# Order of two attention output products, and the place of three weight splits, in a single-core transformer kernel

## What is computed

```
h = rmsnorm(x) * (1 + scale) + shift          # scale, shift from c through w_ada
cq, ckv, k_rope, fq, fk, fv, f_logit, g_mla, g_fox = split(h @ w_in)
o_mla = softmax attention, 8 heads (q and k from cq, ckv through w_uq, w_ukv)
o_fox = forgetting attention, 8 heads (fq, fk, fv, cumulative log gates)
y = sigmoid(g_mla) * (o_mla @ w_o_mla) + sigmoid(g_fox) * (o_fox @ w_o_fox)
x = x + gate_m * (y @ w_out)
```

## Time and profile before

| | |
|---|---|
| runs of the kernel | 1003.09, 1003.9, 1007.6 us; median 1003.9 |
| profiled execution | 1004.27 us, span 1002.5 us |
| TensorE matmul, weight load | 955.7 us (95%), 669.5 us (67%) |
| VectorE, ScalarE, GpSimd | 464.3 us (46%), 378.2 us (38%), 28.3 us (3%) |
| mean granted TensorE clock | 0.993 |
| moved by DMA | 309.37 MB, 309 GB/s on the mean |
| chain that ended last | TensorE 76%, DMA 15%, VectorE 5%, ScalarE 1%, GpSimd 1%, issue 1% |

### The profile page before, as it was taken

How to read it: one execution, slowest core, us unless ns; L and a number is a source line. 1 busy time by engine, 2 the same in 40 slices (tenths; PEclk the granted TensorE clock), 3 DMA queues, 4 the chain that set the end, 5 groups by cost and what they waited for, 6 DMA issues and landing times.

```text
span 1002.5 us, 15338 instructions
## 1 busy us (share of the span) xinstructions
PE 955.7 (95%) x6343; PEld 669.5 (67%) x6343; DVE 464.3 (46%) x860; ACT 378.2 (38%) x718; POOL 28.3 (3%) x60
## 2 busy tenths in 40 slices
PE   7999999898999999999999899999999999898987
PEld 5898778898999999988987434343434344332433
DVE  2797766476787468667875311212121212110113
ACT  2455556554666356454672412121212111110211
POOL 1000000000000000002120000000000000000000
PEclk9999999998999999999999899999999999999999
DMA  9967853633654454534758699999999999999996
GB/s 384 402 266 290 336 203 132 221 120 141 261 187 169 177 204 166 199 138 173 282 218 303 263 430 427 427 427 428 428 428 428 427 428 427 428 427 428 428 425 269
DMA packets 23399, 309.37 MB, mean 309 GB/s; under 512 B 2592, under 2 KB 3104, under 8 KB 4000
## 3 DMA queue, kind: packets, MB, share of 16 engines
q1 hardware_dynamic: 23184, 307.32, 75.3%
q10 hardware_dynamic: 144, 1.05, 0.3%
HBM read 307.31 MB, written 1.05 MB: 308 GB/s over the span
## 4 chain that ended last, share of the span: by engine, by line
PE 76%; DMA 15%; DVE 5%; ACT 1%; issue 1%; POOL 1%; DVEq 0%
PE ps L1001 74%; DMA work<-experts 4%; DMA ring<-experts 4%; DMA slot<-experts 4%; DMA ring<-dense 2%; DVE wl L1656 1%; DMA early<-dense 1%; PE ps L1212 1%; PE ps L1583 1%; DMA colT<-cols 1%; POOL rstd L535 0%; ACT wh L580 0%; PE ps L1525 0%; PE ps L1177 0%; DVE xT L2094 0%
## 5 line engine op out<-in xcount | busy, mean ns | idle before, releaser
L1001 PE MATMUL ps<-hH,wh 128*128 128x256 f32 x704 | 200.3, 284 | 5.1 <-DVE hL L1680 1.9
L1656 DVE TENSOR_TENSOR wl<-ring,wh 128x1024 fp32r<-128x1024 f32 (+1 forms) x136 | 163.7, 1215 | 81.4 <-ACT wh L580 81.1
L1001 PE MATMUL ps<-hL,wh 128*128 128x256 f32 x704 | 197.6, 281 | 0.0
L1001 PE MATMUL ps<-hH,wl 128*128 128x256 f32 x704 | 197.6, 281 | 0.0
L580 ACT ACTIVATE wh<-ring 128x1024 fp32r<-128x1024 f32 (+1 forms) x136 | 140.2, 1042 | 104.0 <-PE ps L1001 95.2
L1001 PEld LDWEIGHTS ps<-hH,wh 128*128 128x128 f32 x704 | 133.3, 189 | 7.8 <-issue 4.3
L1001 PEld LDWEIGHTS ps<-hL,wh 128*128 128x128 f32 x704 | 134.9, 192 | 0.0
L1001 PEld LDWEIGHTS ps<-hH,wl 128*128 128x128 f32 x704 | 133.4, 189 | 0.0
L2363 DVE SCALAR_TENSOR_TENSOR wc<-wc,w_slot,ps 128x512 f32<-128x512 f32 x16 | 12.0, 748 | 221.2 <-PE ps L1001 221.2
L1001 PE MATMUL ps<-aH,wh 128*128 128x256 f32 x304 | 86.1, 283 | 3.6 <-DVE aL L1931 2.9
L1001 PE MATMUL ps<-aL,wh 128*128 128x256 f32 x304 | 85.2, 280 | 0.0
(11 more groups left out here) (351 smaller groups left out, 1424.0 us busy)
## 6 DMA issues: line engine op xcount, KB each, us to landing
ring<-dense SPq DMA_DIRECT2D x39, 2048.0 KB, 7.9
ring<-experts SPq DMA_DIRECT2D x28, 2048.0 KB, 28.2
slot<-experts SPq DMA_DIRECT2D x28, 2048.0 KB, 29.3
work<-experts SPq DMA_DIRECT2D x20, 2048.0 KB, 28.6
early<-experts SPq DMA_DIRECT2D x10, 2048.0 KB, 26.9
wb<-experts SPq DMA_DIRECT2D x9, 2048.0 KB, 25.6
early<-dense SPq DMA_DIRECT2D x4, 2048.0 KB, 8.3
ring<-dense SPq DMA_DIRECT2D x4, 1024.0 KB, 5.4
```

The source lines that it names most:

```text
L1001: return nc.tensor.matmul(o_, l, r, start=start, stop=stop, skip_group_check=True)
L1656: V.tensor_tensor(wl[:, c % CHUNKS, 0:n], src, wh[:, c % CHUNKS, 0:n].bitcast(F32), ALU.subtract)\
```

## The change

Three edits. In the list, and so on TensorE, ScalarE and VectorE, the two halves of `w_o_fox` come before those of `w_o_mla`: the forgetting product is multiplied by its gate into `yF` and the softmax one is added. TensorE's wait for all `o_low` stands now before `om0`, which comes third. Among the gated sums, VectorE splits chunk 1 of `wo0` behind the first low half and only chunk 2 before the second low half, with chunk 3 behind it. At the start, the first chunk of `cq` is split before the tiles on both engines (on ScalarE before its wait for the shift), the tiles 0 to 3 follow in one go, and `keep_warm` is called once, for 8 matmuls, where it was called for 8 and for 9.

```diff
--- before.py
+++ after.py
@@ -135,7 +135,7 @@
     for i, acc in enumerate((2, 0, 0, 0)):
         in_item(f"g{i}", acc)
         ada_item(2, i)
-    for nm, w in (("om", "w_o_mla"), ("of", "w_o_fox")):
+    for nm, w in (("of", "w_o_fox"), ("om", "w_o_mla")):
         for j in range(2):
             half_item(nm, j, w, 4, 512, 2 - 2 * j)
     for j in range(2):
@@ -398,7 +398,7 @@
             if i < 12:
                 split(f"g{1 + i // 4}", i % 4, i % 4 + 1)
             else:
-                split(f"om{(i - 12) // 2}", i % 2, i % 2 + 1)
+                split(f"of{(i - 12) // 2}", i % 2, i % 2 + 1)
 
 
         UNIT_RING = {3: "bg", 5: "w2o_attn", 7: "w2o_conv"}
@@ -615,10 +615,9 @@
             nc.scalar.activation(trig[:, 4], trig[:, 2], ACT.Sin, scale=0.5).then_inc(S("rope_steps"), 1)
             act.wait_ge(S("c_steps"), 2)
             nc.scalar.activation(c_rep[:], ps[:, 2:4, :].rearrange("p a b -> p (a b)"), ACT.Copy).then_inc(S("c_steps"), 1)
+            split("cq", 0, 1)
             act.wait_ge(S("ada_cols"), 1)
-            norm_high(0, adaT[:, SH_M:SH_M + KD], 0, 2)
-            split("cq", 0, 1)
-            norm_high(0, adaT[:, SH_M:SH_M + KD], 2, 4)
+            norm_high(0, adaT[:, SH_M:SH_M + KD], 0, 4)
             split("cq", 1)
             act.wait_ge(S("ada_cols"), 2)
             norm_high(0, adaT[:, SH_M:SH_M + KD], 4, 8)
@@ -731,12 +730,12 @@
                     exps(a + 2)
                 if a >= 2 and a % 2 == 0:
                     o_high(a // 2 - 1)
-            split("om1", 1)
+            split("of1", 1)
             o_high(HEADS - 1)
             for i in range(2):
-                split(f"of{i}")
+                split(f"om{i}")
                 for j in range(2):
-                    v = sig[:, 8 * i + 4 * j:8 * i + 4 * j + 4, :]
+                    v = sig[:, 8 * (1 - i) + 4 * j:8 * (1 - i) + 4 * j + 4, :]
                     act.wait_ge(S("gate_out"), 8)
                     nc.scalar.activation(v, v, ACT.Sigmoid).then_inc(S("sig_ready"), 1)
             split("wo0", 0, 2)
@@ -1112,10 +1111,9 @@
                     mm(ps[:, IT["cq"]["acc"], 0:P], ones, ident[:], True, True)
 
             turn_cols(1, 0, 256)
-            keep_warm(8)
             ada_cols("shift0", 256)
             turn_cols(2, 256, 128)
-            keep_warm(9)
+            keep_warm(8)
 
             h_in = ("norm_in", [IN_BASE[0] + k + 1 for k in range(KD)])
             chunk("cq", 0, hH, hL, True, ready=h_in)
@@ -1248,15 +1246,15 @@
                     elif a + i < N1 - 2:
                         ada_part(2, 1 + a // 4)
                 values(a)
+            linear("of0", aH[:, 4:8], aL[:, 4:8], False)
+            ada_turn(4)
+            pe.wait_ge(S("gate_out"), 8)
+            linear("of1", aH[:, 4:8], aL[:, 4:8], False)
+            pe.wait_ge(S("of_out"), 2)
             pe.wait_ge(S("o_low"), HEADS)
             linear("om0", aH, aL, False)
-            ada_turn(4)
-            pe.wait_ge(S("gate_out"), 8)
+            pe.wait_ge(S("of_out"), 4)
             linear("om1", aH, aL, False)
-            pe.wait_ge(S("om_out"), 2)
-            linear("of0", aH[:, 4:8], aL[:, 4:8], False)
-            pe.wait_ge(S("om_out"), 4)
-            linear("of1", aH[:, 4:8], aL[:, 4:8], False)
             y_low = ("y_low", [1] * 4 + [2] * 4)
             pe.wait_ge(S("y_ready"), 2)
             linear("wo0", hH, hL, False, ready=y_low)
@@ -1781,9 +1779,8 @@
             scaled(0, KD)
             cols_out(2, 256, 128, "ada_shift0", SH_M).then_inc(S("ada_cols"), 1)
             dve.wait_ge(S("ada_cols"), 1)
-            shifted_low(0, 2)
             split("cq", 0, 1)
-            shifted_low(2, 4)
+            shifted_low(0, 4)
             split("cq", 1)
             cols_out(3, 384, 128, "ada_shift2", SH_M + 4).then_inc(S("ada_cols"), 1)
             dve.wait_ge(S("ada_cols"), 2)
@@ -1953,30 +1950,31 @@
                 done(f"{name}{i}")
                 for j in range(2):
                     m = 4 * i + 2 * j
-                    dve.wait_ge(S("sig_ready"), i + 1 + (2 if name == "of" else 0))
+                    dve.wait_ge(S("sig_ready"), i + 1 + (2 if name == "om" else 0))
                     src = ps[:, IT[f"{name}{i}"]["acc"] + j, :].rearrange("p (a b) -> p a b", a=2)
-                    if name == "om":
-                        V.tensor_tensor(yF[:, m:m + 2, :], sig[:, m:m + 2, :], src, ALU.mult).then_inc(S("om_out"), 1)
+                    if name == "of":
+                        V.tensor_tensor(yF[:, m:m + 2, :], sig[:, 8 + m:10 + m, :], src, ALU.mult).then_inc(S("of_out"), 1)
                     else:
-                        link(V.tensor_tensor(sig[:, 8 + m:10 + m, :], sig[:, 8 + m:10 + m, :], src, ALU.mult))
-                        V.tensor_tensor(yF[:, m:m + 2, :], yF[:, m:m + 2, :], sig[:, 8 + m:10 + m, :], ALU.add)\
+                        link(V.tensor_tensor(sig[:, m:m + 2, :], sig[:, m:m + 2, :], src, ALU.mult))
+                        V.tensor_tensor(yF[:, m:m + 2, :], yF[:, m:m + 2, :], sig[:, m:m + 2, :], ALU.add)\
                             .then_inc(S("y_ready"), 1)
 
-            split("of0")
-            o_proj("om", 0)
+            split("om0")
+            o_proj("of", 0)
             ada_out(2, 4)
             V.scalar_tensor_tensor(out=scale_f[:], in0=adaT[:, SC_F:SC_F + KD], scalar=1.0,
                                    in1=colT[:, ROW["ffn_g"]:ROW["ffn_g"] + KD], op0=ALU.add, op1=ALU.mult)\
                 .then_inc(S("ada_cols"), 1)
-            split("of1")
-            o_proj("om", 1)
-            dve.wait_ge(S("om_out"), 4)
+            split("om1")
+            o_proj("of", 1)
+            dve.wait_ge(S("of_out"), 4)
             for i in range(2):
-                o_proj("of", i)
-                split("wo0", i, 3 * i + 1)
+                o_proj("om", i)
+                split("wo0", 2 * i, 2 * i + 1)
                 dve.wait_ge(S("y_high"), 4 * i + 4)
                 V.tensor_tensor(hL[:, 4 * i:4 * i + 4, :], yF[:, 4 * i:4 * i + 4, :], hH[:, 4 * i:4 * i + 4, :].bitcast(F32),
                                 ALU.subtract).then_inc(S("y_low"), 1)
+                split("wo0", 2 * i + 1, 2 * i + 2)
             split("wo1", 0, 3)
 
             def residual(m, src, scale, sem):
```

## The result

| | kernel before | changed kernel |
|---|---|---|
| median (16 executions each) | 1002.93 us | 993.47 us |
| lowest to highest | 998.70 to 1007.88 | 991.67 to 1002.08 |
| mean | 1003.10 | 994.56 |
| profiled execution | 1004.27 | 1002.08 |
| its span | 1002.5 | 1000.3 |

The ratio is 0.9904, with an interval of 0.9882 to 0.9926: 9.5 us faster by the medians, 8.5 by the means. The forecast was 999.2 us with a range from 996.8 to 1002.2. The direction was right, the size was not, and the time lies outside the range.

A forecast was written before the change was run, and what follows sets the result against it. The end belongs to DMA, but the long expert stream starts when TensorE releases it, so TensorE's earlier gains count. Profile 1004.27 less 2.9 + 1.8 + 0 = 4.7 gives 999.6, less 0.4 gives 999.2 us; range 996.8 to 1002.2.

The forecast's parts named there:

- The swap: Ahead of the first output product: forgetting product first removes TensorE's wait for the last o_low, gaining 2.9 us.
- the one on the clock: Products after the 2.91 us gap at 185 still step by 0.118 us, so no clock fall was assumed.
- The splits: In w_out's first half: fewer VectorE splits ahead of the second low half bring TensorE's third chunk 1.8 us sooner.
- The start: At the kernel's start: earlier first split and fewer warm-ups gain 0, at most 1.15 us, as VectorE awaits the modulation load.
- a granted clock of 0.5 between 28 and 45 us: Sign of being wrong: missing warm-up halves TensorE's clock on the first weights; over 0.5% slower had chance 0.05.
- To the end one for one: Whatever TensorE gains before expert unit 10's issue at 566 us moves the expert stream and the end by as much.
- The rival of the expert stream: The final expert weight loads swallow the gain, leaving 1003.9 us; chance 0.04.
- The sum: Whole kernel: gains of 2.9 + 1.8 + 0 = 4.7 us.
- one low stretch: TensorE at half speed from about 242.6 to 247.4 us, costing 2.4; it could vanish (996.8) or grow as much (1001.6).
- the swap alone with a clock stretch that grows: High end of the range, 1002.2 us; the swap alone paying was a rival at 1001.0, chance 0.12.
- start and clock together: Low end of the range, 996.8 us: the start pays too and the low clock stretch near 242 us vanishes.
- D: Theory of the follow-up runs: matmuls run at 113.3 or 117.8 ns, and the change makes the faster pace likelier.

The follow-up runs named there:

- b2_split_only: Kernel before with only w_out's splits moved around the low halves: median 1000.63 us, ratio 0.9991.
- c4_gap_back: Changed kernel with TensorE's old wait for all low halves put back ahead of the first output product: median 999.77 us, ratio 0.9966 against the kernel before.
- a1_change_again: Changed kernel executed again, unaltered: median 994.44 us, ratio 0.9938 against the kernel before.
- b1_swap_only: Kernel before with only the order of the two output products swapped: median 998.92 us, ratio 0.9977.
- b4_norm_warm: Changed kernel with 4 and 7 warm-up matmuls added in the two waits of the middle norm: median 997.68 us, ratio 0.9964 against the kernel before.
- b3_gap_warm: Kernel before with 11 warm-up matmuls filling the idle 2.9 us ahead of the first output product: median 1001.79 us, ratio 1.0000.
- c1_change_third: Changed kernel executed a third time, unaltered: median 996.00 us, ratio 0.9928 against the kernel before.

## Why the prediction was wrong in size

**The swap: its length right, the clock behind it left out.** The step "gain 187.72 - 184.81 = 2.9 us" priced the gap at its length, and its length is what the traces give back, 2.98. The step that failed is the one on the clock, which put nothing on what follows the gap: "the gap at 185 does not call for it". It read one execution, in which the clock held, as the rule. In two of five profiles with the gap the clock falls right after it and the products take 1.6 to 1.7 us longer, and every kernel with the gap has a lower mean clock than every kernel without. The Trainium skill ("TensorE: Matmul & The Clock Gate", section "Loop structure matters more than you think") had the right sign here: its long wait that makes TensorE cold is seen in `b2_split_only` and `c4_gap_back`, and not in the other three. I had turned its warning on the start, which had a cover, and away from the gap, which had none.

**The splits: right.** Forecast 1.8 us with 0.2 of a gap left. The gap is 0.16 in `a1_change_again` and in `b2_split_only` (0.36 in the changed kernel's first profile, whose first two chunks ran at the faster pace). The third chunk comes 6.02 us after the first, where 5.8 was named, so the gain is 1.6.

**The start: right at 0.** VectorE gets the modulation block at 43.95 to 44.50 us in the profiles with the edit and at 43.81 to 44.39 in the others. It waits for it for 3.1 to 5.7 us in the former and 2.8 to 6.3 in the latter, so the cover was there every time. The prediction named a granted clock of 0.5 between 28 and 45 us as a sign of being wrong. It came in three profiles, and the load covered it.

**To the end one for one: right.** From unit 10's issue to the end it is 436.0 to 436.8 us in twelve of the fourteen profiles and 437.8 in two (`b1_swap_only`, `b4_norm_warm`), early or late alike: that issue lies between 556.06 and 566.88. In the three profiles of the change it is at 564.16, 556.06 and 563.89, where 561.5 was named. The rival of the expert stream falls.

**The sum.** The two edits give 2.98 + 1.6 = 4.6 us, where 4.7 were forecast. (The stretch from `wo1` to unit 0 takes 65.97 us on the mean of the changed kernel and its two repeats, 65.68, 65.77 and 66.47, against 71.15 of before. That is 5.2, and what exceeds 4.6 is pace and low stretches.) The other part of the answer is the clock. Its mean over all executions of before in the three batches is 0.9873, over the change's 40 it is 0.9893. A mean of 0.002 more is 4 us less at half speed, and those are worth at most 2 us of work. 4.6 and up to 2 make up to 6.6; the gain measured over the three comparisons is 8.5, 6.9 and 6.5, and 7.1 on the mean of all six that hold both swap and splits. The 0.5 us between 6.6 and 7.1 lies within the intervals. That the clock gives the 2 us is worked out from means and was not shown by a run, since `b3_gap_warm` left it open. By the falls seen in the profiles, two in five, it would be 0.7. What of the first comparison's 9.5 lies above that stays open too; two repeats came out lower.

**The range.** It took the kernel before as 1003.9, on three runs and one profile, with a spread only of the steps that were edited and of one low stretch. Beside the changed kernel the kernel before had a median of 1002.93, so 1.0 of the 5.7 us by which the forecast missed is this base. In 105 further executions beside the batches that kernel ran from 997.74 to 1012.91. Two sources of spread lie in stretches that the edit doesn't touch, the pace (6.4 us) and the clock falls (1.7 us or more each). The profile of before had the pace of 117.8 ns in the feed-forward layer, which four of fourteen profiles have, but fewer clock falls than most (mean clock 0.993 against 0.987). These nearly cancelled, so its time looked typical. Nor do the two ends follow from the terms: the swap alone with a clock stretch that grows is 1001.0 + 2.4 = 1003.4, not 1002.2, and start and clock together are 999.2 - 1.15 - 2.4 = 995.6, not 996.8. Even 995.6 lies above the 993.47 measured.

**D is not borne out.** In the feed-forward layer the pace of 117.8 ns stands in two of the six profiles without both swap and splits (the first one of before, and `b3_gap_warm`), and in two of the eight with them (the changed kernel's first and `c1_change_third`). A small shift can't be told from so few. The pace explains why two profiles differ by 2.2 us where the medians differ by 9.5: not the gain but what one looks at.

## What to carry to other kernels

Price a gap on the critical path at its length and, apart from that, ask what the clock does behind it in several executions: one profile in which it holds proves nothing. Before two profiles are compared, cut both into segments at marks that the code sets (DMA issues that wait for progress) and compare each segment; one that no edit touches tells whether the executions are alike. Where a segment differs, look at TensorE's own instructions before the edit is given the difference, since the pace can change at a wait: here it made 3.7 us out of 2.98. An edit on an engine that waits for a load later on is worth nothing until the load comes earlier, and may even take a warm-up away without cost.

## What the hardware showed that was not expected

**Two paces at the same granted clock.** The pace was first seen in the feed-forward layer. From about 242 to 432 us TensorE runs some 1,650 matmuls (128x256, one weight load each) without a break. In ten of fourteen profiled executions they step by 113.3 ns, in the other four by 117.8 ns, from the first to the last. The segment from unit 0 to units 1 and 2 takes 223.1 us or 229.5 where the clock held near 440, and 224.7 to 226.3 or 231.1 to 231.3 where it fell there. There is nothing between. The granted clock reads 1.00, the releasers and the order are the same, and both versions of the code show both. The products ahead of it show both too, and one execution can change from one to the other at a wait: w_out goes at 117.8 ns in nine profiles and at 113.3 in five, the output products at 117.8 in the first profile of before alone. What chooses the pace stays open; no run tried to find it.

The Trainium skill ("TensorE: Matmul & The Clock Gate", section "Back-to-back issue gap") gives N/2.4 + 2.5 ns for an isolated matmul at the full clock, an estimate of 109 ns for 256 columns, and says that in a stream the weight loads set the distance too, with 81 ns measured for 128 columns and 131 for 512. Both paces measured here lie between these two, and above the 109.

**Clock falls come and go.** Near 240 us, in the middle norm, the clock falls in every profile; near 440 us in nine of fourteen; after the 2.9 us gap in two of five. It is low near 550 us in all fourteen. The mean clock of single executions varies accordingly, and so does their time.
